# First modulation computed in quarters of 256 columns, with a token-wise first norm, in a two-block transformer kernel

## What is computed

```python
c_act = silu(c)                                  # 1024
mod   = c_act @ ada_w + ada_b                    # 1024 x 6144 weights, 24 MB
sh1, sc1, g1, sh2, sc2, g2 = split(mod, 6)
h     = rms_norm(x, norm1_g) * (1 + sc1) + sh1   # 512 x 1024
proj  = h @ w_in + b_in                          # 18 column blocks of 128
```

## Time and profile before

| | |
|---|---|
| median of three runs | 1997.86 us |
| the profiled execution, its own time | 1995.88 us |
| its span | 1994.1 us |
| mean granted TensorE clock | 0.993 |
| PE, DVE, ACT, POOL busy | 97%, 52%, 40%, 9% |
| waits of PE from 60 to 500 us | six kinds, 0.3 to 1.5 us in all each |

### The profile page before, as it was taken

The page is one execution under the profiler, slowest core; times in us unless marked ns, Lnnn a source line. Parts: engine busy times, 40 slices in busy tenths (PEclk is TensorE's granted clock), DMA queues, the critical chain, the costliest instruction groups (busy, mean ns, idle before and its releaser), DMA issues.

```text
span 1994.1 us, 35178 instructions
## 1 busy us (share of the span) xinstructions
PE 1940.5 (97%) x14503; PEld 1576.1 (79%) x14503; DVE 1041.4 (52%) x1509; ACT 798.0 (40%) x1217; POOL 173.5 (9%) x191
## 2 busy tenths in 40 slices
PE   6999999999999999999999999999999999999999
PEld 5777778888887687787778788888868887888887
DVE  6788765555324755778845534432265465343312
ACT  4345243333224545777634332322245353223222
POOL 1100000000014000000001111111100001111010
PEclk8999999999999999999999999999999999999999
DMA  9545223333323132000012233333222223333331
GB/s 320 180 137 148 85 74 95 95 97 114 107 84 82 57 97 84 11 12 8 8 58 75 85 101 98 95 116 101 58 74 80 88 82 89 95 96 106 108 102 43
DMA packets 313904, 181.60 MB, mean 91 GB/s; under 512 B 18717, under 2 KB 306611, under 8 KB 313780
## 3 DMA queue, kind: packets, MB, share of 16 engines
q1 hardware_dynamic: 308354, 162.82, 27.4%
q0 software_dynamic: 4608, 16.78, 2.7%
q10 hardware_dynamic: 818, 0.21, 0.0%
HBM read 177.69 MB, written 2.10 MB: 90 GB/s over the span
## 4 chain that ended last, share of the span: by engine, by line
PE 86%; DVE 6%; ACT 4%; issue 3%; ACTq 1%; POOL 0%; DVEq 0%; POOLq 0%
PE bank L261 23%; PE bank L263 23%; PE bank L262 23%; PE bank L2409 4%; DVE wlo L246 1%; PE bank L1333 1%; PE bank L1335 1%; PE bank L612 1%; PE bank L1334 1%; PE bank L2939 1%; PE bank L3046 1%; ACT whi L239 0%; ACTq L807 0%; PE bank L2944 0%; PE bank L2963 0%
## 5 line engine op out<-in xcount | busy, mean ns | idle before, releaser
L246 DVE TENSOR_TENSOR wlo<-raw,whi 128x1024 fp32r<-128x1024 f32 (+1 forms) x251 | 327.4, 1304 | 644.4 <-ACT whi L239 644.4
L239 ACT ACTIVATE whi<-raw 128x1024 fp32r<-128x1024 f32 (+1 forms) x251 | 280.6, 1119 | 636.6 <-PE bank L263 630.1
L261 PE MATMUL bank<-fh_hi,whi 128*128 128x512 f32 x991 | 387.6, 391 | 5.0 <-DVE wlo L246 3.5
L262 PE MATMUL bank<-fh_lo,whi 128*128 128x512 f32 x991 | 386.3, 390 | 0.0
L263 PE MATMUL bank<-fh_hi,wlo 128*128 128x512 f32 x991 | 386.1, 390 | 0.0
L261 PEld LDWEIGHTS bank<-fh_hi,whi 128*128 128x128 f32 x991 | 186.3, 188 | 46.0 <-DVE wlo L246 4.6
L263 PEld LDWEIGHTS bank<-fh_hi,wlo 128*128 128x128 f32 x991 | 186.4, 188 | 39.1
L262 PEld LDWEIGHTS bank<-fh_lo,whi 128*128 128x128 f32 x991 | 186.4, 188 | 39.1 <-issue 0.5
L261 PE MATMUL bank<-f_hi,whi 128*128 128x512 f32 x528 | 205.7, 390 | 0.0
L263 PE MATMUL bank<-f_hi,wlo 128*128 128x512 f32 x528 | 205.4, 389 | 0.0
L262 PE MATMUL bank<-f_lo,whi 128*128 128x512 f32 x528 | 205.4, 389 | 0.0
(11 more groups left out here) (522 smaller groups left out, 3172.5 us busy)
## 6 DMA issues: line engine op xcount, KB each, us to landing
raw<-in_w_up_dram SPq DMA_DIRECT2D x44, 512.0 KB, 3.7
raw<-in_ffn_w_gate_dram SPq DMA_DIRECT2D x44, 512.0 KB, 3.7
raw<-in_ffn_w_up_dram SPq DMA_DIRECT2D x44, 512.0 KB, 3.7
raw<-in_ffn_w_down_dram SPq DMA_DIRECT2D x32, 704.0 KB, 4.0
late<-in_ada_w_dram POOLq DMA_DIRECT2D x32, 512.0 KB, 4.1
raw<-in_rwkv_w_rkv_dram SPq DMA_DIRECT2D x24, 512.0 KB, 3.4
raw<-in_w_down_dram SPq DMA_DIRECT2D x16, 704.0 KB, 4.0
early<-in_ada_w_dram SPq DMA_DIRECT2D x16, 512.0 KB, 14.0
```

The lines of the kernel that those rows point to most:

```text
L239: act.activation(halves_of(at)[0][:, 0:kts * P], raw_unit(at, kts), ACT.Copy).then_inc(hi_ready, 1)
L246: dve.tensor_tensor(lo[:, 0:kts * P], raw_unit(at, kts), hi[:, 0:kts * P].bitcast(F32), ALU.subtract)\
L261: pe.matmul(dst, hi, rhs_hi(k), start=first and k == 0, stop=False)
L262: pe.matmul(dst, hi, rhs_lo(k), start=False, stop=False)
```

## The change

The two early parts (shift and scale) are cut into four *quarters*. Quarter q holds columns 256q to 256q+255 of both parts, that is, what tiles 2q and 2q+1 of `h` need. Each is loaded as eight blocks of 128x2x256, computed, added up, and turned into `mod` and `gain` by itself, and tiles 2q and 2q+1 are made behind it. PE takes four of the eight blocks of quarter 0 and three of the others; its products have 32 moving columns instead of 1.

The first norm's squares are summed per token by ACT (four activations over 128x1024 with an accumulator); root and reciprocal are 128x4; PE spreads the result over the partitions and ACT copies it out. The product `x * rstd` moves to POOL, eight tiles; ACT applies gain and shift in one pass and makes `h_hi` in a second; DVE makes only `h_lo`.

SP's list becomes: `x_tok`, quarter 0, units 0 and 1, quarters 1 to 3 (quarter 2 waits for the first sum, quarter 3 for the last transpose), unit 2 and on. `pool_late` waits for the last quarter's sums. Of `vrow`'s loads, the eleven that fill its first block go out on ACT's queue ahead of its first table load, and 16 move to POOL's. The late accumulation's ten blocks in the first units shift from (1,2,2,2,2,1) to (0,2,2,2,2,2).

```diff
-    ON_PE = (2, 5, KD + 1)
+    NQ_ADA, QW = 4, 2 * P
+    ON_PE = ((1, 3, 5, 7), (1, 3, 7), (1, 3, 7), (1, 3, 7))
...
+    def sp_quarter(sp, q):
+        if q == 2:
+            sp.wait_ge(ada_sum, 1)
+        if q == 3:
+            sp.wait_ge(x_turned, KD)
...
+        def act_tile(self, act, k):
+            act.wait_ge(tmp_ready.sem, self.t0 + k + 1)
+            if k % 2 == 0:
+                act.wait_ge(gain_ready.sem, GAIN0 + k // 2 + 1)
+            act.activation(self.slot(k), self.slot(k), ACT.Identity, scale=gain[:, k:k + 1], bias=mod[:, k:k + 1])\
+               .then_inc(nhi_ready.sem, 1)
+            act.wait_ge(nhi_ready.sem, self.hi0 + 2 * k + 1)
+            act.activation(h_hi[:, k, :], self.slot(k), ACT.Copy).then_inc(nhi_ready.sem, 1)
...
+    def pe_rows(pe, q, rows_):
+        for m in rows_:
...
+            for i, a, j in ada_columns(q):
+                pe.matmul(quarter_bank(q)[:, i * ADA_SPAN:(i + 1) * ADA_SPAN],
+                          ada_block(q)[:, m, a, j * P:(j + 1) * P], cact[:, m:m + 1].to_broadcast([P, ADA_SPAN]),
+                          start=m == ON_PE[q][0] and i == 2 * q, stop=False, skip_group_check=True)
...
+    def pe_first_units(pe):
+        pe_rows(pe, 0, ON_PE[0])
+        pe_quarter_sums(pe, 0)
+        norm1.pe_spread(pe)
+        for k in range(2, KD):
+            pe_turn_x(pe, k)
+        pe_turn_vecs(pe)
+        pe_spread(pe)
+        wait(pe, x_ready.sem, KD)
+        for step in range(KD + LAG):
+            q, second = divmod(step, 2)
+            if q + 1 < NQ_ADA:
+                pe_rows(pe, q + 1, ON_PE[q + 1][second:second + 1])
+            for u, k in ((0, step), (1, step - LAG)):
+                if 0 <= k < KD:
+                    if u == 0:
+                        split1.pe_ready(pe, k)
+                    unit_products(pe, at_in[u], KD, bank[u][:, :], lambda k_: h_hi[:, k_, :], lambda k_: h_lo[:, k_, :],
+                                  True, True, ks=[k])
+            if second and q + 1 < NQ_ADA:
+                pe_rows(pe, q + 1, ON_PE[q + 1][2:])
+                pe_quarter_sums(pe, q + 1)
...
     def act_mixer1(act):
-        norm1.act_root(act)
+        act_copy_x(act, 2)
+        act_copy_x(act, 3)
+        split1.act_tile(act, 0)
+        split_hi(act, first[0])
+        split1.act_tile(act, 1)
+        for k in range(4, KD):
+            act_copy_x(act, k)
+        split_hi(act, first[1])
+        act_vecs(act)
         act_angles(act)
...
-        for n in range(len(BY_DVE)):
...
+        for q in range(1, NQ_ADA):
+            dve_rows(dve, q, ON_DVE[q])
+            if q == 1:
+                split_lo(dve, first[1])
+            dve_quarter_mod(dve, q)
+            split1.dve_lo(dve, 2 * q)
+            split1.dve_lo(dve, 2 * q + 1)
```

More of the change, by code:

```diff
@@ L688, in landed_at @@
         return slot_count[at.raw_slot] + more * 16 + at.i * (at.step // RAW * 16)
-    ON_PE = (2, 5, KD + 1)
-    BY_DVE = [m for m in range(EARLY) if m not in ON_PE]
+    NQ_ADA, QW = 4, 2 * P
+    ON_PE = ((1, 3, 5, 7), (1, 3, 7), (1, 3, 7), (1, 3, 7))
+    ON_DVE = [[m for m in range(KD) if m not in rows_] for rows_ in ON_PE]
     def ada_used(m):
@@ L772, in build @@
     setup.close()
+    early_x = sbs(setup, "early_x", [P, KD, 2, QW])
+    setup.close()
     late = sbs(setup, "late", [P, RAW, D])
@@ L858, in pe_setup, with pe_turn_x, pe_turn_vecs @@
         pe.wait_ge(x_landed, 16 * NT)
[L859 to L869, removed]
+        for k in range(2):
+            pe_turn_x(pe, k)
+        pe.wait_ge(small_landed, SMALL)
+        pe.transpose(bank[5][:, 0:P], vrow[:, 0, :], ident[:, :]).then_inc(small_turned, 1)
+    SMALL = 16 * (3 + len(VEC_FIRST))
+    def pe_turn_x(pe, k):
+        wait(pe, x_ready.sem, k - 1)
+        for t in range(NT):
+            tr = pe.transpose(bank[k % 2][:, t * P:(t + 1) * P], x_tok[:, t, k * P:(k + 1) * P], ident[:, :])
+        tr.then_inc(x_turned, 1)
+    def pe_turn_vecs(pe):
+        pe.wait_ge(vec_landed, 16 * len(VEC_REST))
+        for b in range(1, VB):
             m = P if b < VB - 1 else LAST_ROWS
@@ new lines, in pe_quarter_sums, with dve_quarter_mod @@
+    def pe_quarter_sums(pe, q):
+        pe.wait_ge(ada_done, sum(len(ON_DVE[i]) for i in range(q + 1)))
+        for i, a, j in ada_columns(q):
+            mm = pe.matmul(quarter_bank(q)[:, i * ADA_SPAN:(i + 1) * ADA_SPAN],
+                           ada_quarter(q)[:, (2 * a + j) * P:(2 * a + j + 1) * P], ones[:, 0:ADA_SPAN],
+                           start=False, stop=True, skip_group_check=True)
+        mm.then_inc(ada_sum, 1)
+    def dve_quarter_mod(dve, q):
+        dve.wait_ge(ada_sum, q + 1)
+        if q == 0:
+            dve.wait_ge(vecs_ready, 1)
+        ks = slice(2 * q, 2 * q + 2)
+        both = lambda t_: t_.rearrange("p (a k) -> p a k", a=2)[:, :, ks]
+        dve.tensor_tensor(both(mod[:, 0:2 * KD]), both(quarter_bank(q)[:, ::ADA_SPAN]),
+                          both(vecs[:, col["ada_b"]:col["ada_b"] + 2 * KD]), ALU.add).then_inc(ada_evac, 1)
+        dve.wait_ge(ada_evac, q + 1)
+        dve.scalar_tensor_tensor(gain[:, ks], mod[:, KD + 2 * q:KD + 2 * q + 2], 1.0,
+                                 vecs[:, col["norm1"] + 2 * q:col["norm1"] + 2 * q + 2], ALU.add, ALU.mult)\
+           .then_inc(gain_ready.sem, 1)
@@ L3782, in _ @@
         pool_setup(pool)
+        pool_vecs(pool)
+        for k in range(KD):
+            split1.pool_normed(pool, k)
         pool_late(pool)
```

214 lines of the change are left out of this document (130 added, 84 removed).

## The result

The changed kernel takes 2021.54 us (median of four runs, 2018.67 to 2021.77); the kernel before, run beside it, 1997.34 (1996.63 to 1997.87). The ratio is 1.0118, 95% interval 1.0101 to 1.0136: slower, by some 24 us. The profiled execution took 2021.39 us for a span of 2019.7.

A forecast was written before the change was run, and what follows sets the result against it. PE's chain of waits up to the rotation (58.95 us) was taken as the bound; low-clock steps gave +24.3, a held clock +17. The middle, +20.5, made 2016.4, plus 1.98 to the median: 2018 us, range 2004 to 2026.

The forecast's parts named there:

- Step 1: Setup up to quarter 0's sum: small loads delay DVE's cast by 1.6 us to 10.3; first sum ends at 22.4.
- Step 2: First tile, through norm spread, POOL's product, ACT's two passes and DVE's low half: there at about 29.2 us.
- Step 3: Before quarter 1: ACT's list from 27.0 delivers the sines at 37.6 us; PE waits, finishing their spread at 38.9.
- Step 4: Quarter 1: 12 products, 4 sums and two triples at the low clock take 9.5 us, to 48.4.
- Step 5: Quarters 2 and 3: each waits 2.8 us after a sum, then small products and triples; ends 60.4 and 73.7.
- Step 6: Tail: 2.8 us and seven triples, clock rising behind three of them; ends at 83.2, +24.3 against 58.95.
- The choice of +20.5: Stretch up to the rotation: middle between +24.3 and +17, the latter if the clock rises at 54 to 57 and holds.
- What costs nothing: Transfers of quarters 2 and 3 and later units land before use; one more late block costs 0 to 1.3 us.
- POOL against DVE: Norm products moved to POOL: the skill's rule gives 6 us more, the rows only tile 0's 0.5 to 1.5.
- High clock throughout: Rival for PE before the rotation: 32 columns hold 2.4 GHz, periods 8.8, rotation 65.0, +6, 2004 us; chance 0.12.
- PE low "until the triples": PE before the first triple: all work is narrow, so the clock stays at 0.50 until triples have run.

The follow-up runs named there:

- wide products: Changed kernel plus 256-column products of a constant tile, results unused, where PE waits: 2010.49 us with 114, 2007.5 us with 138.
- the one-round kernel: Changed kernel with all products and sums of quarters 1 to 3 run before the first triple: 2008.95 us.
- the kernel with all rows on DVE: Changed kernel with DVE accumulating all eight blocks in quarters 1 to 3, PE only doing the sums: 2022.26 us.
- 50 in the other: Kernel before with whole modulation, token-wise norm and rearranged loads and blocks, plus 50 unused 256-column products: 1995.23 us, ratio 0.999.
- the kernel with the token-wise norm: Kernel before, modulation whole, with the change's token-wise norm and rearranged loads and blocks: 1993.3 us once, median 1996.77 us of eleven runs, ratio 0.9995.

## Why the prediction was right

The forecast was 2018.0 with a range of 2004 to 2026, slower with 0.89; it came to 2021.5. The cause was the one named, and the steps stand as follows.

- *Step 1, first sum at 22.4*: it ended at 24.6. The miss is the cast, taken at 10.3 within 8.7 to 12.6 and measured at 12.71, a little above the upper bound: the semaphore did wait for the last of the small loads. Products and sums cost 0.43 as said (6.88 for 16). Freeing the positions brought the 3.3 us back.
- *Step 2, first tile at 29.2*: 31.5 (30.04 + 1.46). It was late with the cast, POOL's product was quicker than taken (1.28 for 1.6), and the low half twice as long (1.46 for 0.75). The low half did not matter, as said, because of step 3; the late cast did, since ACT's list starts behind it, and 3.3 us taken off the cast brought the rotation 3.3 earlier.
- *Step 3, the sines*: 37.69 (forecast 37.6), their spread over at 39.0 (38.9). PE waited for line 1024, as named. **That the time fits is luck:** ACT began this list at 28.5 and not at 27.0, and took 9.2 us for it and not 10.6. Part of that shorter time is the eight transposes in it, which ran at the high level; with them at the low one it took 10.0, and the sines came at 38.5. Either miss alone would have put the sum off by about 1.5 us.
- *Step 4*: quarter 1's sums ended at 48.55 (48.4).
- *Step 5*: 59.3 and 72.8 (60.4 and 73.7). The first is shorter because the clock rose inside it.
- *Step 6*: 83.52 (83.2). The tail took 10.7 where 9.5 was taken, because the clock rose behind five adjacent triples and not three.
- *The choice of +20.5* between 24.3 and 17 is **the term that was mis-sized**. It supposed that the clock, once up behind the triples at 54 to 57, might hold. It did rise there, but PE then waited for bias, ACT and low half (60 to 62 us), and it was at 0.50 again until 81.9. The sum at the low clock, 24.3, was right to 0.3 us, with the two misses of steps 1 and 3 offsetting each other and the late tail (step 6) against the short period (step 5).
- *What costs nothing*: no load was waited for behind quarter 0, as said. The late block ahead of the first softmax cost 0.75 (0 to 1.3, 0.5 taken).
- *POOL against DVE*: only the first tiles' were to count, 0.5 to 1.5 us. POOL's product was 1.27 against 0.68 on DVE. With the Trainium skill, "GPSIMD Engine Reference" (4.1 Engine selection), two-input operations are about twice as slow there: the trace agrees (1.9 times). What its rule would have made of it, 6 us in all, did not come: 0.1 to 0.3 us at the sums, once the earlier cast is taken off. The price that neither looked at, DVE's own longer work beside POOL, was hidden behind PE at the low clock; it showed only where the wide products held the high one.
- *High clock throughout*, +6: with it held by wide products the rotation was still at 70.3, not 65. Thirty-two columns did not lift it: the 48 products and sums in one row (the one-round kernel) ran at 0.43 from the first to the last. And the period of 8.8 at the high clock was 10.4, for DVE's low half and block beside POOL.
- *PE low "until the triples"* was not strictly so: eight transposes at 28 us, and eight at 33, took 1.14 in all, 0.14 each, the high level, with no wide sums anywhere. The later ones were worth 0.8 us at the sines, as the kernel with all rows on DVE shows, in which they ran low.

## What to carry to other kernels

Work split into quarters so that the first tile can start sooner pays only if the last tile's inputs are not later for it: here the first triple came 4.9 us earlier and the last 24.6 us later, since each quarter added its own wait of 3 us (bias, gain, two ACT passes, low half), and since TensorE stayed at 1.2 GHz through nearly all of it. Look for what a finer interleaving does to the clock: count the stretch twice, at both levels; here the sum at the low one was the right one, and a rise between two waits did not last. Look for a gain of 0.2% in where a fixed step starts in the trace, but follow the difference back to the step at which it begins: one rotation came 2.7 us earlier, and 1.0 of that was a load that happened to land sooner. And take more runs than a few: a single execution of 1993.3 belonged to a median of 1996.8.

## What the runs showed of the hardware

- *POOL and DVE hold each other up.* DVE's subtraction over 128x512 took 0.69 alone and 1.29 to 1.75 beside a POOL product of the same shape; that product took 1.27 where nothing held it and 2.12 beside DVE. An accumulation of 512 columns took 0.75 alone and 1.61 beside it. The times of the changed kernel fit one that waits for the other and not two that share: low halves that began at 30.04, 51.90 and 62.98, within a POOL product, each ended 0.55 us behind the end of that product (30.95, 52.64, 64.09), and POOL's long one, begun at 31.64, ended 1.1 us behind DVE's weight split (32.63). Handing a two-input operation to an idle POOL is not free for DVE.
- *Accumulations in a chain* on DVE came every 0.86 us for a duration of 0.75.
- *Wide products did not always lift the clock.* 114 and 138 of them held it for most or all of 28 to 71 us in the changed kernel, but 50 in the other did not: from 24 to 42 us PE was busy throughout, with small products and 24 of the wide ones, at 0.50, and the wide ones only lengthened the row.
- *The high level was lost around the waits, more than once.* Besides 60 to 62 us in the changed kernel, it was so in the kernel with the later spread of the sines: quarter 3's sums ended at the high level at 67.72, and the triples behind the wait, from 70.45 on, ran at 0.43 a product.
- *The clock column can be wrong before its first change.* In the single execution of the kernel with the token-wise norm it reads 1.00 from 34 to 50 us, although its products of a triple came 0.43 apart until 49.6; there the durations decide.
